# The first gate/up block from X transposed before its norm, and 32 bytes more ahead of the phase regions

## The reference, cut to what matters

```python
def swiglu_ffn(h, w13, w2):
    gate, up = jnp.split(h @ w13, 2, axis=-1)
    return (jax.nn.silu(gate) * up) @ w2

# first_block, DEPTH = 1
x = x + 0.5 * swiglu_ffn(rms_norm(x, ffn1_norm[l]), ffn1_w13[l], ffn1_w2[l])   # where the kernel starts
h = rms_norm(x, mix_norm[l]); proj = h @ w_in[l]                               # convolution and attention, mixer 1
x = x + y @ w_out[l]
x = x + 0.5 * swiglu_ffn(rms_norm(x, ffn2_norm[l]), ffn2_w13[l], ffn2_w2[l])
x = rms_norm(x, final_norm)
# second_block, two layers: gated delta rule (mixer 2), stick-breaking attention (mixer 3),
# after each one a SwiGLU and h + (p @ ple_w_proj) * sigmoid(rms_norm(h) @ ple_w_gate)
```

## Time and profile before

| | us |
|---|---|
| three runs, median | 1241.16 (1239.9 to 1241.28) |
| the profiled execution, its own time | 1241.24 |
| its span, from the first to the last instruction | 1239.5 |
| TensorE matmuls busy | 1227.9, 99% of the span |
| VectorE busy | 787.6 |
| ScalarE busy | 617.4 |
| GpSimd busy | 74.1 |

### The profile page before, as it was taken

How to read it: one execution, slowest core, us unless ns; L and a number is a source line. 1 busy time by engine, 2 the same in 40 slices (tenths; PEclk the granted TensorE clock), 3 DMA queues, 4 the chain that set the end, 5 groups by cost and what they waited for, 6 DMA issues and landing times.

```text
span 1239.5 us, 16166 instructions
## 1 busy us (share of the span) xinstructions
PE 1227.9 (99%) x6414; PEld 1046.2 (84%) x6414; DVE 787.6 (64%) x936; ACT 617.4 (50%) x786; POOL 74.1 (6%) x123
## 2 busy tenths in 40 slices
PE   8999999999999999999999999999999999999998
PEld 7888888998888888899999888888888888888887
DVE  4766536897655655677777666654677756655545
ACT  5544436665544433645623544444456765445333
POOL 1000002002000000400001000000013100000000
PEclk9999999999999999999999999999999999999999
DMA  8997755451588774544301488876265437887640
GB/s 272 317 278 243 235 187 165 167 179 62 185 266 241 237 256 135 189 154 152 105 1 47 124 277 262 240 239 207 95 251 195 162 93 240 254 258 229 226 136 34
DMA packets 172307, 235.33 MB, mean 190 GB/s; under 512 B 13800, under 2 KB 127560, under 8 KB 172232
## 3 DMA queue, kind: packets, MB, share of 16 engines
q1 hardware_dynamic: 172232, 234.30, 58.9%
HBM read 221.67 MB, written 12.58 MB: 189 GB/s over the span
## 4 chain that ended last, share of the span: by engine, by line
PE 91%; DVE 6%; ACT 1%; POOL 1%; DMA 0%; issue 0%; SPq 0%; DVEq 0%; ACTq 0%; POOLq 0%
PE bank L1605 27%; PE bank L1607 27%; PE bank L1606 27%; DVE y L1183 3%; PE bank L1997 2%; DVE wlo L1066 2%; PE bank L2008 1%; PE bank L1639 1%; PE bank L1970 1%; PE bank L1963 1%; PE bank L1924 1%; PE bank L2016 1%; DMA raw<-in_ffn_w_dram 0%; PE bank L2113 0%; PE bank L2135 0%
## 5 line engine op out<-in xcount | busy, mean ns | idle before, releaser
L1066 DVE TENSOR_TENSOR wlo<-raw,whi 128x2048 fp32r<-128x2048 f32 (+1 forms) x190 | 416.0, 2194 | 247.3 <-ACT whi L431 247.2
L431 ACT ACTIVATE whi<-raw 128x2048 fp32r<-128x2048 f32 x190 | 363.0, 1915 | 227.6 <-PE bank L1607 218.7
L1605 PE MATMUL bank<-whi,xThi 128*128 128x512 f32 x1024 | 402.0, 393 | 2.2 <-DVE xTlo L1547 0.8
L1607 PE MATMUL bank<-whi,xTlo 128*128 128x512 f32 x1024 | 399.1, 390 | 0.0
L1606 PE MATMUL bank<-wlo,xThi 128*128 128x512 f32 x1024 | 398.7, 389 | 0.0
L1605 PEld LDWEIGHTS bank<-whi,xThi 128*128 128x128 f32 x1024 | 192.3, 188 | 43.2 <-DVE xTlo L1547 1.4
L1607 PEld LDWEIGHTS bank<-whi,xTlo 128*128 128x128 f32 x1024 | 192.2, 188 | 40.4
L1606 PEld LDWEIGHTS bank<-wlo,xThi 128*128 128x128 f32 x1024 | 192.4, 188 | 39.1
L1605 PE MATMUL bank<-whi,hThi 128*128 128x512 f32 x352 | 139.4, 396 | 0.0
L1606 PE MATMUL bank<-wlo,hThi 128*128 128x512 f32 x352 | 139.1, 395 | 0.0
L1607 PE MATMUL bank<-whi,hTlo 128*128 128x512 f32 x352 | 139.0, 395 | 0.0
(11 more groups left out here) (389 smaller groups left out, 1139.3 us busy)
## 6 DMA issues: line engine op xcount, KB each, us to landing
raw<-in_ffn_w_dram SPq DMA_DIRECT2D x176, 256.0 KB, 4.4
raw<-in_ffn_w_in_dram SPq DMA_DIRECT2D x176, 256.0 KB, 4.1
raw<-in_ffn_w_dram SPq DMA_DIRECT2D x22, 1024.0 KB, 5.3
raw<-in_ffn_w_out_dram SPq DMA_DIRECT2D x22, 1024.0 KB, 5.3
raw<-in_gdn_w_in_dram SPq DMA_DIRECT2D x16, 1024.0 KB, 5.3
hidden<-hblk SPq DMA_DIRECT2D x44, 256.0 KB, 5.1
hraw<-hidden SPq DMA_DIRECT2D x176, 64.0 KB, 3.6
raw<-in_w_in_dram SPq DMA_DIRECT2D x10, 1024.0 KB, 5.1
```

The lines of the kernel that those rows point to most:

```text
L431: act.activation(whi[w % SPLIT][:], raw[w % RAW][:], ACT.Copy).then_inc(w_hi, 1)
L1066: dve.tensor_tensor(wlo[w % SPLIT][:, c], raw[w % RAW][:, c], whi[w % SPLIT][:, c].bitcast(F32), ALU.subtract).then_inc(w_lo, 1)
L1605: pe.matmul(psum, lhs[0], rhs[0], start=start, stop=False, skip_group_check=True)
L1607: return pe.matmul(psum, lhs[1], rhs[0], start=False, stop=stop, skip_group_check=True)
```

## The change

`gain_col` ([128, 8], 32 bytes per partition) is declared ahead of the regions, and `row_gain` ([8, 128]) at the end of one of them. The regions now begin at byte 150,016.

The norm n0 leaves the list of turns. SP loads X's first tile, the gain row as 8 rows of 128, and X's second tile, all ahead of the weights. TensorE runs 14 warm-up products, turns the gain rows into a column in bank 3, and turns X itself, both row tiles, into banks 4 to 7, where a bank holds two groups of 128 columns of D for all 256 rows. ScalarE's `first_hi(k)` copies one group (256 columns) with the gain as its scale pointer, VectorE's `first_lo(k)` makes gain times the bank less `xThi` in one instruction. These alternate with the pieces of the weights. `first_block` goes through the eight groups, each with both row tiles. The sums of the squares stand behind the second slot's pieces on ScalarE, and the root comes in behind the product: as the scale pointer of Silu and as the scalar in VectorE's product, for the first SwiGLU alone. The third slot is also split piece by piece. The diff, cut to the lines that change and their neighbours:

```diff
--- before.py
+++ after.py
@@ -42,7 +42,7 @@
     RAW, SPLIT = 4, 4
-    WARM = 11
+    WARM = 14
     PE_TAPS = 6
@@ -107,11 +107,11 @@
     ROOT_D = math.isqrt(D)
-    gain_before = {"up0": [0], "mix": [1], "up1": [2], "gdn": [3, 4], "up2": [5], "ple_p0": [6],
+    gain_before = {"mix": [1], "up1": [2], "gdn": [3, 4], "up2": [5], "ple_p0": [6],
                    "kv": [7, 8], "up3": [9], "ple_p1": [10]}
 
-    TURN = ["n0", "n1", "n2", "n4", "gdn", "n5", "n6", "n7", "n8", "n9", "n10"]
-    turn_of_up = ["n0", "n2", "n5", "n9"]
+    TURN = ["n1", "n2", "n4", "gdn", "n5", "n6", "n7", "n8", "n9", "n10"]
+    turn_of_up = [None, "n2", "n5", "n9"]
 
@@ -174,6 +174,7 @@
         GDNG, KG, QG = range(3)
+        gain_col = sb("gain_col", [P, KD])
         sb("level", [P, 40])
@@ -188,12 +189,12 @@
             gate_s = lent.enter_context(nc.sbuf_tensor("gate_s", [P, NT, D], F32))
-        hThi, hTlo, hnat, hblk, hraw, p_in, pThi, pTlo, pp, row_tap, row_tap4 = region(
+        hThi, hTlo, hnat, hblk, hraw, p_in, pThi, pTlo, pp, row_tap, row_tap4, row_gain = region(
             [("hThi", [P, NBLK, 4, P], F32R), ("hTlo", [P, NBLK, 4, P], F32R),
...
              ("pp", [P, NT, D], F32)],
-            [("row_tap", [P, P], F32), ("row_tap4", [W4 * QKV, P], F32)])
+            [("row_tap", [P, P], F32), ("row_tap4", [W4 * QKV, P], F32), ("row_gain", [KD, P], F32)])
 
@@ -271,14 +272,14 @@
         for w, pieces in enumerate(slots):
-            if w >= 2:
+            if w >= 3:
                 total[w % RAW] += 16 * len(pieces)
...
 
-        FIRST, PIECES = 2, 4
+        FIRST, PIECES = 3, 4
 
@@ -300,6 +301,9 @@
             return 4 * m + 2 * t + b + 1
+
+        def gain_done(n):
+            return sem(f"gain_in{n % 2}"), 16 * (n // 2 + n % 2)
 
@@ -349,15 +353,18 @@
             for w, pieces in enumerate(slots):
-                if w < NT:
-                    sp.dma_start(X[:, w, :], a["x"][0, w * P:(w + 1) * P, :]).then_inc(sem(f"x_in{w}"), 16)
+                if w == 0:
+                    for t in range(NT):
+                        sp.dma_start(X[:, t, :], a["x"][0, t * P:(t + 1) * P, :]).then_inc(sem(f"x_in{t}"), 16)
+                        if t == 0:
+                            sp.dma_start(row_gain[:], NORM[0].rearrange("(k p) -> k p", p=P)).then_inc(sem("first_gain"), 16)
                 for name, s0 in first.items():
...
                             sp.wait_ge(sem("final_x"), NT)
-                        elif n >= 2:
+                        elif n > 2:
                             sp.wait_ge(sem("turn_in"), turned_in(f"n{n - 2}", 1))
@@ -435,9 +442,8 @@
                 act.wait_ge(ready, value - (not whole))
-                i = turn(f"n{max(n, 4) if n == FINAL else n}")
-                if i and n not in (FINAL, FINAL + 1):
-                    act.wait_ge(sem("turn_T"), 4 * (i - 1) + 2 * t + 2)
+                if n > 1 and n not in (FINAL, FINAL + 1):
+                    act.wait_ge(sem("turn_T"), 4 * (turn(f"n{n}") - 1) + 2 * t + 2)
                 if n == FINAL + 1:
@@ -512,8 +518,10 @@
                             act.wait_ge(sem("ffn_blk"), NBLK * f + j - 1)
-                        act.activation(hnat[:, j % 2, t, :], bank[2 * (j % 2) + t][:, 0:256],
-                                       ACT.Silu).then_inc(sem("ffn_silu"), 1)
+                        if f == 0:
+                            act.wait_ge(sem("norm_rstd"), nth(0, t))
+                        act.activation(hnat[:, j % 2, t, :], bank[2 * (j % 2) + t][:, 0:256], ACT.Silu,
+                                       scale=1.0 if f else rstd[:, t:t + 1]).then_inc(sem("ffn_silu"), 1)
                     split(s + 2 + SPLIT)
@@ -879,23 +887,24 @@
 
-            def first_hi(t, b):
-                act.wait_ge(sem("turn_T"), 2 * t + b + 1)
-                act.activation(xThi[:, 4 * b:4 * b + 4, t * P:(t + 1) * P], bank[4 + b][:].rearrange("p (k c) -> p k c", k=4),
-                               ACT.Copy).then_inc(sem("turn_hi"), 1)
-
-            norm_sum(0, 0, sem("x_in0"), 16)
-            piece_hi(0, 0)
-            piece_hi(0, 1)
-            first_hi(0, 0)
-            piece_hi(0, 2)
-            first_hi(0, 1)
-            piece_hi(0, 3)
-            norm_sum(0, 1, sem("x_in1"), 16)
-            for k in range(PIECES):
-                piece_hi(1, k)
-            first_hi(1, 0)
-            first_hi(1, 1)
+            def first_hi(k):
+                act.wait_ge(sem("first_T"), k + 2 - k % 2)
+                if k == 0:
+                    act.wait_ge(sem("first_col"), 1)
+                act.activation(xThi[:, k, :], bank[4 + k // 2][:, (k % 2) * SEQ:(k % 2 + 1) * SEQ], ACT.Copy,
+                               scale=gain_col[:, k:k + 1]).then_inc(sem("first_hi"), 1)
+
+            first_hi(0)
+            first_hi(1)
+            for n in range(KD // 2 - 1):
+                piece_hi(0, n)
+                first_hi(2 * n + 2)
+                first_hi(2 * n + 3)
+            for n in range(KD // 2 - 1, FIRST * PIECES):
+                piece_hi(n // PIECES, n % PIECES)
+                if n == 2 * PIECES - 1:
+                    norm_sum(0, 0, sem("x_in0"), 16)
+                    norm_sum(0, 1, sem("x_in1"), 16)
             ffn(0)
@@ -1073,7 +1082,7 @@
                 c = 2 * (7 if n == 8 else n) + t
-                dve.wait_ge(sem(f"gain_in{n % 2}"), 16 * (n // 2 + 1))
+                dve.wait_ge(*gain_done(n))
                 if n == FINAL + 1:
@@ -1144,8 +1153,12 @@
                         dve.wait_ge(sem("ffn_silu"), 2 * (NBLK * f + j) + t + 1)
-                        dve.tensor_tensor(hnat[:, j % 2, t, :], hnat[:, j % 2, t, :],
-                                          bank[2 * (j % 2) + t][:, 256:512], ALU.mult).then_inc(sem("ffn_h"), 1)
+                        h, up = hnat[:, j % 2, t, :], bank[2 * (j % 2) + t][:, 256:512]
+                        if f:
+                            dve.tensor_tensor(h, h, up, ALU.mult).then_inc(sem("ffn_h"), 1)
+                        else:
+                            dve.scalar_tensor_tensor(out=h, in0=up, scalar=rstd[:, t:t + 1], in1=h,
+                                                     op0=ALU.mult, op1=ALU.mult).then_inc(sem("ffn_h"), 1)
                     split(s + 2 + SPLIT)
@@ -1534,35 +1547,23 @@
 
-            def first_scale(t, b):
-                c = slice(b * 512, (b + 1) * 512)
-                dve.wait_ge(sem("norm_rstd"), nth(0, t))
-                dve.wait_ge(sem("gain_in0"), 16)
-                dve.scalar_tensor_tensor(out=xs[:, t, c], in0=X[:, t, c], scalar=rstd[:, t:t + 1], in1=gain[0][:, c],
-                                         op0=ALU.mult, op1=ALU.mult).then_inc(sem("turn_in"), 1)
-
-            def first_lo(t, b):
-                part = (slice(None), slice(4 * b, 4 * b + 4), slice(t * P, (t + 1) * P))
-                dve.wait_ge(sem("turn_hi"), 2 * t + b + 1)
-                dve.tensor_tensor(xTlo[part], bank[4 + b][:].rearrange("p (k c) -> p k c", k=4), xThi[part].bitcast(F32),
-                                  ALU.subtract).then_inc(sem("turn_lo"), 1)
-
-            first_scale(0, 0)
-            first_scale(0, 1)
-            piece_lo(0, 0)
-            piece_lo(0, 1)
-            first_lo(0, 0)
-            piece_lo(0, 2)
-            first_lo(0, 1)
-            piece_lo(0, 3)
-            piece_lo(1, 0)
-            piece_lo(1, 1)
-            first_scale(1, 0)
-            piece_lo(1, 2)
-            first_scale(1, 1)
-            piece_lo(1, 3)
-            first_lo(1, 0)
-            first_lo(1, 1)
+            def first_lo(k):
+                dve.wait_ge(sem("first_hi"), k + 2 - k % 2)
+                dve.scalar_tensor_tensor(out=xTlo[:, k, :], in0=bank[4 + k // 2][:, (k % 2) * SEQ:(k % 2 + 1) * SEQ],
+                                         scalar=gain_col[:, k:k + 1], in1=xThi[:, k, :].bitcast(F32),
+                                         op0=ALU.mult, op1=ALU.subtract).then_inc(sem("first_lo"), 1)
+
+            dve.wait_ge(sem("first_gain_T"), 1)
+            dve.tensor_copy(gain_col[:], bank[3][:, 0:KD]).then_inc(sem("first_col"), 1)
+            dve.wait_ge(sem("first_col"), 1)
+            first_lo(0)
+            first_lo(1)
+            for n in range(KD // 2 - 1):
+                piece_lo(0, n)
+                first_lo(2 * n + 2)
+                first_lo(2 * n + 3)
+            for n in range(KD // 2 - 1, FIRST * PIECES):
+                piece_lo(n // PIECES, n % PIECES)
             ffn(0)
@@ -1575,7 +1576,7 @@
                 dve.wait_ge(sem("turn_T"), 4 * (turn("n4") - 1) + 2 * t + 2)
-                dve.wait_ge(sem(f"gain_in{FINAL % 2}"), 16 * (FINAL // 2 + 1))
+                dve.wait_ge(*gain_done(FINAL))
                 dve.tensor_tensor(xs[:, t, :], X[:, t, :], gain[FINAL % 2][:], ALU.mult).then_inc(sem("final_g"), 1)
@@ -1778,7 +1779,7 @@
                     block_rows(up_slot(f, j), xT, [bank[2 * (j % 2) + t] for t in range(NT)],
```

(47 more changed lines are left out.)

## The result

The changed kernel takes 1233.52 us (median of 5 runs, 1232.78 to 1233.94), the kernel before 1241.27 beside it (1239.9 to 1241.33): ratio 0.9939, 95% interval 0.9926 to 0.9953. The forecast was 1232.6. The profiled execution of the changed kernel took 1233.52, with a span of 1231.8. Most of these kernels have executions with a stretch of 3.4 us at a lower clock and others, some 1.5 us shorter, without it (for the kernel before about 1241.3 and 1239.9), and a median of a few can be of either kind.

The account below looks back on a forecast made before the run. The prediction took TensorE, busy for 99% of the span, to bound the kernel. Its gains of 8.0 (regions) and 0.6 (start) made 8.6, from 1241.24 to 1232.6 us; the range was 1230.0 to 1236.5.

Parts of the forecast that it names:

- Term 1: Regions moved to byte 150,016: 1,200 matmuls on operands in them each lose 6.7 ns, 8.0 us in all.
- a multiple of 64 (and of 256): Where the regions begin after the change; both operands at multiples of 64 were to give the 226.7 ns pace.
- the mismatch with the moving operand: Possibility for matmuls on the regions: unlike placement of both operands costs, not a high address alone; left undecided.
- Term 2: First block's new start: second block's first matmul at 23.4 instead of 24.03, gaining 0.6 us (0.1 to 0.8).
- a risk ahead of the first Square: ScalarE, third slot: a table load of 1.28 there would make it ready at 23.7, 0.3 late.
- The third slot's pieces: Weight pieces behind both norms: ScalarE done at 21.5, VectorE at 22.4, needed at 23.4.
- the fifth slot: Load lands at 28.65, remainder done by 33.0, needed by the third block at 34.3, so hidden.
- waits ahead of the mixers: Where the regions' gain might be given back, which would show the prediction wrong; no size given.
- (a): Rival on the regions: their place is not the cause, only the start's gain is left, 1240.6; chance 0.11.
- (b): Clock rival, first blocks: one slow stretch costs 1.6, 1234.2 (chance 0.06); 1.2 GHz through two blocks, 1251.8 (0.03).
- the slow stretch at 537 falls away with its new timing: Case for the 1.2 GHz stretch from 537.4 to 540.8: its disappearance saves 1.5 us, allowed for in the range.

Follow-up runs that it names:

- the 96-byte kernel: The kernel before with an unused tensor of 96 bytes ahead of the regions, which then begin at byte 150,080: 1241.2 us, ratio 1.0001.

## Why the prediction was right

**Term 1, the regions: right in size, its condition wrong.** 1,200 matmuls at 6.7 ns were to give 8.0, and the ledger gives 7.85, all of it where it was to be. The 32 bytes alone bring 7.6 to 7.7, with 0.3 given back as below. But "a multiple of 64 (and of 256)" was the wrong property. What the change does is to bring the regions, which began 32 below a multiple of 256, level with the weights modulo 256; the multiple of 64 in the change's name fails by itself (1241.2), and no multiple is needed (1232.66 with all at 32 past one). The prediction had it as a possibility, "the mismatch with the moving operand", and read it out of the earlier trace rows, where both operands are alike and cheap; it did not need to decide.

The Trainium skill's SBUF — State Buffer, Operand start alignment, calls its rule one of legality, not speed, and says that its runs timed nothing. The prediction made of that a rule by which the shift gives 0, which is more than the page says. Over this kernel a start 32, 64 or 128 off costs 5.7 to 6.7 ns of each matmul of 512 columns, and the measurement decides.

**Term 2, the start: right in sign, 0.2 instead of 0.6.** The step that failed is the first matmul of the first block, put at 12.3 and found at 12.74. The rows that it used were right: copies 0.37 apart (0.38 foreseen), VectorE's steps 0.40 apart, a piece's remainder 0.60, no stops behind the first. What was missing is the table load of 1.28. I had placed one as a risk ahead of the first Square, much later; it came ahead of the first Copy, and not at 0.78 as in the earlier trace rows, where nothing stands before it, but behind the first wait. With the load moved the first matmul is at 12.30 and the second block's at 23.37, as predicted. The third slot's pieces (VectorE done at 22.48) and the fifth slot were in time, as costed.

**What was not in the sum: 0.3 given back** behind the second `down` product. The norm that follows is hidden by that product's last matmuls. VectorE's part of it starts 3.31 earlier than before, here in the changed kernel and then in the kernel before:

```profile
480.50 1.23 DVE L1580 TENSOR_TENSOR xs<-X,gain 128x1024 f32<-128x1024 f32 x1
```

```profile
483.81 1.23 DVE L1579 TENSOR_TENSOR xs<-X,gain 128x1024 f32<-128x1024 f32 x1
```

It follows on a bank behind which 48 matmuls of that product are still to come. The last matmul ahead of the transposes starts 3.62 earlier, since those 48 last 0.32 less, and the gap grows by that. The gap is 0.96 to 1.01 in all eight traces in which the regions are level with the weights, with the old start and the new, and 0.56 to 0.74 in the other six. The prediction named the place ("waits ahead of the mixers") as something that would be wrong, but priced it at nothing.

Together 7.85 + 0.2 - 0.3 is the ledger's 7.75, against 8.6 in the prediction. Its 1232.6 is 0.9 below the measured 1233.5: 0.4 by the table load, 0.3 by the cover, and the rest by term 1 and rounding.

**The rivals.** (a) fell with the 32 bytes alone. (b) fell too: TensorE stood for 2.25 (12.74), longer than the 1.8 feared, and the granted clock read 1.00 in all of the first two blocks. With 7 warm-ups it stood 1.69 and the clock was at 1.00 as well. The case that "the slow stretch at 537 falls away with its new timing", 1.5 us and the lower end of the range, had the size right; the reason, the new timing, is not shown, for the kernel before already has executions with the stretch and without. The traces of both kernels have it.

## What to carry to other kernels

Where matmuls of one shape run at two paces, compare the SBUF starts of their moving and their stationary operand modulo 256, before looking at code or queues; an unused tensor of a few bytes (32 here) is both the test and the cure, and a change elsewhere that declares a small tensor may move the time by it. Where a stage of TensorE gets faster, what it covered has to be taken off the gain. A table load is issued where its first user stands, behind that user's waits: put it ahead of them (0.44 us here). Where a stretch at a lower clock comes in some executions only, look at the single times before reading a difference of two medians or two traces: 1.5 us of one difference here were only that.

## What was not expected of the hardware

- **A matmul pays for unlike starts.** 128x512 in fp32r: 226.7 ns with equal starts modulo 256, 233.3 with 32 (either way) or 64 off, 232.4 with 128 off. Why is open; only the pace was measured.
- **At 256 columns it goes the other way.** In the kernel with the weights moved, where the roles are exchanged (`xThi`/`xTlo` moving, `whi`/`wlo` stationary), the form `xTlo,whi` takes 282 ns, against 285 in the 96-byte kernel, whose weights and `xThi` are level:

```profile
L1607 PE MATMUL bank<-xTlo,whi 128*128 128x256 f32 x288 | 82.1, 285 | 0.0
```

  From start to start it is 119.3 against 122.4 ns, a mean over 855 that takes in the stretch at 1.2 GHz in both, 2.6 us in all. In the ledger of that kernel against the kernel before, the 2,976 newly slow matmuls cost 18.3 (6.2 ns each) and these give back 2.6; the last matmul is 15.8 later. Why 256 columns gain is open.
- **A stretch at the 1.2 GHz level, 3.4 us long, comes in some executions of a kernel and not in others.** It lies between 530 and 547 in the traces of both kernels and of ten experiments, and in neither of the other two, whose kernels have other executions 1.0 to 1.8 us longer. Ahead of it stands a group of 24 matmuls of 1 to 8 columns that takes 2.5 us: each of the twelve stretches begins 0.1 to 1.3 us after the last of them has started. It costs 1.5 us. What decides whether it comes was not tested.
- **The clock also comes up at another time in each execution.** With the same eleven warm-ups, the traces of the kernel before and of the one with 32 bytes more have their warm-ups and first transposes 0.21 us apart until 8.35 and until 5.67; from there on they come 0.11 apart, and the granted clock reads 1.00.
